# Two passes instead of three for the 64-row token tile of a hybrid trunk, and token reloads behind the last output unit

## The chip, the cores and the metric

The kernel runs on one core of a Trainium2 chip. The metric is the device time of one execution in microseconds, the median over runs. Everything is float32 in memory; the large projections are made of products in the fp32r format, which the code calls a high part and a rest.

## What is computed

One inference step of a one-layer trunk for 512 prompt tokens and 64 sample tokens, model width 1024. Cut to what matters here:

```python
u = rmsnorm(h, g_mix)
proj = u @ w_in                       # q, k, v, LRU input and gate, z, x/B/C, dt (8 columns)
o_a = stick_breaking(q, k, v)         # attention without softmax
o_b = rglru_branch(...)               # gated linear recurrence
o_c = ssd_branch(...)                 # Mamba-2 scan, gated with silu(z)
gates = sigmoid(u @ w_gate + b_gate)
merged = gates[0] * (o_a @ wbo[:512]) + gates[1] * (o_b @ wbo[512:1024]) + gates[2] * (o_c @ wbo[1024:])
h = h + merged @ w_out
h = h + hier_moe(rmsnorm(h, g_ffn))   # router: 1 of 4 groups, 2 of its 8 experts; 32 SwiGLU experts
y = rmsnorm(h, g_final)
```

## The kernel before

The 576 tokens are five tiles (`TT`): four of 128 rows and the last, tile 4, of 64. An operand of a large projection is split on the chip: `u_high_r` is `u` rounded to fp32r and `u_rest_r` what is left; weights likewise (`high_r`, `rest_r`). A product then takes three matmuls for each of the eight 128-row slices `k` of the contraction, in `product` (lines 790 to 794): high by high, high by rest, rest by high.

The projections are one list of work items (`ITEMS`, lines 107 to 130), which TensorE runs in that order into the two banks of `pj`: item n uses bank n % 2 and waits until item n-2 has been drained. The kinds that matter here: `v` (a token tile as the stationary operand, 512 weight columns moving), `z` and `o` (a token tile stationary, 256 columns), `dt` (8 weight columns stationary, 288 tokens moving). Tile 4 has one `v` item, two `z` items and four `o` items, written below as o(4,0) to o(4,3). `DRAINED` says which engine drains: ScalarE takes `v`, `z` and `dt`, VectorE takes `k`, `b` and `o`.

Other steps (`JOBS`) are hung between the items: attention in the stretch of the x, r, gb and z items, then the LRU and SSD mixers, and between the `o` items the second norm (`ffn_norm`), its transposes (`ffn_turn`), the router's logits and the picking of experts. Each engine walks the same list of jobs and items in order, so a VectorE step is behind every VectorE step of earlier items. After the last `o` item come what is left of the routing (`ranks`, `hots`, `table`, `slots`, `weights`), a gather of token rows on the GpSimd queue, and 16 pairs of experts whose matrices stream from HBM.

SyncE's queue (lines 640 to 762) issues the loads: weight units of 128 columns into four ring slots, each issue waiting for the item that frees its slot. Around the `o` items it issues the second four output units (`OUTU` to `OUTU+3`, q = 2 and 3 of the `o` items), the reload of token tile 0, of tiles 1 to 4 (`reload_x`), and the first two gate matrices, in the order

```python
if u == OUTU + 2:
    sp.wait_ge(S["pj_full"], IDX[("g", KD - 1, 1, 2)] + 1)
    reload_x(0)
...
for t in range(1, NT):
    reload_x(t)
...
load("gate", None, 0, EPAIRS)
sp.wait_ge(S["pj_full"], NITEM)
load("up", None, 0, EPAIRS)
```

Each unit that has landed is split by ScalarE (line 1327, high) and VectorE (line 1736, rest). `reload_x` brings the residual rows back into `h`, to which the drain of an `o` item adds (line 1796). GpSimd's `ffn_norm(0)` (line 2541) fetches the row of gains `g_ffn`, which VectorE needs at line 2021.

Of the kernel before, what the change touches and what calls it, by code (L numbers as in the profile page):

```python
# [27 lines left out]
P = 128  # L28
D = 1024
SEQ = 512  # L30
DEC = 64
# [50 lines left out]
SMALL = 1312  # L82
# [48 lines left out]
DVE_KINDS = ("k", "b", "o")  # L131
IDX = {}
# [41 lines left out]
for _it in ITEMS:  # L174
    _e = 1 if _it[0] in DVE_KINDS else 0
    _cnt[_e] += 1
    DRAINED.append((_e, _cnt[_e]))

ATT = [("p", hp, kb) for hp in range(PAIRS) for kb in reversed(range(KB))]
# [105 lines left out]
def trunk_and_experts(nc, a, o):  # L285

    ctx = ExitStack()
    with ctx:
# [124 lines left out]
        xp = [at(x, 584) for x in xp_off]  # L413
        v_sb = at(merged_off, NT, W)
# [41 lines left out]

        wexp_off = front
# [76 lines left out]
        w_dt_h = tiny(KD * 8)  # L534
# [17 lines left out]
        w_dt_hr = region("w_dt_high_r", small, KD * 8).rearrange("p (k n) -> p k n", k=KD)  # L552
        w_dt_rr = region("w_dt_rest_r", w_dt_off, KD * 8).rearrange("p (k n) -> p k n", k=KD)
# [28 lines left out]
        def last_bank(k):  # L582
# [6 lines left out]
            route_ps route_in routed mix_high mix_rest vp_in consts gmix_in ut_u ut_h high_r rest_r v_rest_p wdt_r  # L589
# [51 lines left out]
        def _(sp):  # L641
# [122 lines left out]
        def _(pe):  # L764
# [30 lines left out]

            def item(n):
# [4 lines left out]
                if kind == "v":  # L801

                    pe.wait_ge(S["ut_r"], hh + 1)
                s = SLOT.get(u)
# [19 lines left out]
                elif kind == "o":  # L824
# [4 lines left out]
                    for k in range(KD):  # L829
                        if n == OUT0:  # L830
                            pe.wait_ge(S["mix_rest"], NMIX + 2 * k + 1)
                        mh, mr = (x[k // 2][:, k % 2, o0:o0 + rows_n] for x in (merged_high, merged_rest))
                        m = product(out, (mh, mr), (pair_r(s, 1, k), pair_r(s, 0, k)), k)
                elif kind == "v":
                    o0, rows_n = TT[hh]
                    for k in range(KD):
                        if hh == 0 and k % 2 == 0:
                            j = k // 2
                            pe.wait_ge(*((S["rest_r"], j + 1) if j < NVD else (S["v_rest_p"], j - NVD + 1)))
                        uh, ur = (x[:, k, o0:o0 + rows_n] for x in (u_high_r, u_rest_r))  # L840
                        m = product(bank[0:rows_n, :], (uh, ur), (v_high[:, k, :], v_rest[:, k, :]), k)
                elif kind == "z":
                    o0, rows_n = TT[hh]
                    out = bank[0:rows_n, 0:256].rearrange("p (a b) -> p a b", a=2)
                    for k in range(KD):
# [97 lines left out]
            def att_values(u):  # L943
                kind, hp, kb = ATT[u]
                w = att_a[u % 2]
                if u == 0:
                    wait_drained(pe, IDX[("v", 0, NT - 1)])
                    pe.wait_ge(S["vp_in"], 16)
# [350 lines left out]
        def _(act):  # L1299
# [43 lines left out]
            def params(_):  # L1343
# [3 lines left out]
                act.activation(w_dt_hr, w_dt, ACT.Copy).then_inc(S["wdt_r"], 1)  # L1347
# [4 lines left out]

            def item(n):
                it = ITEMS[n]
                kind, c, hh = it[:3]
                if kind in DVE_KINDS:
# [17 lines left out]
                elif kind == "dt":  # L1374
                    if hh == 0:
                        act.wait_ge(S["xt_ps"], NT)
                    m = act.activation(dtT[0:8, lo:lo + HALF], bank[0:8, 0:HALF], ACT.Copy)
# [30 lines left out]
                if n == IDX[("v", 0, NT - 1)]:  # L1408
                    act.wait_ge(*drained(n))
                    act.dma_start(o["v_p"][0, 0].rearrange("(t p) h d -> p t (h d)", p=P),  # L1410
                                  v_sb[:, 0:NT - 1, :]).then_inc(S["v_out"], 16)
                    act.dma_start(o["v_s"][0, 0].rearrange("s h d -> s (h d)"),
                                  v_sb[0:DEC, NT - 1, :]).then_inc(S["v_out"], 16)
# [275 lines left out]
        def _(dve):  # L1689
# [60 lines left out]
            def params(_):  # L1750
                par_half()
                dve.wait_ge(S["wdt_r"], 1)
                dve.tensor_tensor(w_dt_rr, w_dt, w_dt_hr, ALU.subtract
# [12 lines left out]
            def item(n):  # L1766
                it = ITEMS[n]
                kind, c, hh = it[:3]
                if kind not in DVE_KINDS:
# [3 lines left out]
                lo = hh * HALF  # L1773
                if kind == "k":
# [15 lines left out]
                elif kind == "o":  # L1790
                    t, q = c, hh
                    r = TT[t][1]
                    if q == 0:
# [3 lines left out]
                                                 op0=ALU.mult, op1=ALU.add)  # L1797
                m.then_inc(S["pj_dve"], 1)
# [553 lines left out]
        def _(pool):  # L2352
# [52 lines left out]

            pool.wait_ge(S["xt_ps"], NT)
# [220 lines left out]
```

## Time and profile before

| | |
|---|---|
| median of 3 runs | 1193.73 us (1193.71, 1193.73, 1196.59) |
| the profiled execution's own time | 1197.67 us |
| its span in the profile | 1195.9 us |
| TensorE busy | 1115.6 us (93%) |
| VectorE, ScalarE, GpSimd busy | 532.3, 329.3, 220.7 us |
| mean granted TensorE clock | 0.974 of 2.4 GHz |
| HBM read | 258.24 MB |

Times in the rows are microseconds from the start of the span. The profile models the end of a matmul, so matmuls overlap in it: what one costs is the distance from its start to the next start. A bracket at the end of a row is the idle time before it and what ended that.

### The profile page before, as it was taken

The numbers are of one execution on the slowest core, as the hardware profiler recorded it, in microseconds if no ns is written. First come the engines' busy times: TensorE is split into PE (matmuls) and PEld (weight loads), VectorE is DVE, ScalarE is ACT, GpSimd is POOL, SyncE is SP. The second block draws the span as 40 slices with busy tenths as digits, with TensorE's granted clock in tenths as the row PEclk, the third lists the DMA queues.
The fourth block names the chain that finished last, engine by engine and source line by source line (L and its number), as shares of the span: only waits on it lengthen the run. The fifth ranks groups of instructions, "written<-read, shape, count | busy, mean of one in ns | idle before, by whom it ended". The sixth has DMA issues, their size and how long they took to land.

```text
span 1195.9 us, 16868 instructions
## 1 busy us (share of the span) xinstructions
PE 1115.6 (93%) x6713; PEld 790.2 (66%) x6713; DVE 532.3 (45%) x990; ACT 329.3 (28%) x555; POOL 220.7 (18%) x232
## 2 busy tenths in 40 slices
PE   5999999999999999999999879999999989998994
PEld 4799877779989899999989743344334333333431
DVE  4331787763257555534435631343333333232335
ACT  3323444444366444433321101111111111111113
POOL 6000423333513446532200000000000000000000
PEclk8999999999999999999999869999999999999997
DMA  9278544463312112353280399999999999999982
GB/s 191 77 126 113 51 53 49 52 53 38 94 53 67 59 54 63 89 138 97 76 287 39 147 361 429 401 415 428 428 428 426 426 429 427 427 427 428 427 344 81
DMA packets 93292, 263.15 MB, mean 220 GB/s; under 512 B 5021, under 2 KB 73849, under 8 KB 80937
## 3 DMA queue, kind: packets, MB, share of 16 engines
q1 hardware_dynamic: 86640, 250.36, 61.0%
q0 software_dynamic: 3456, 6.58, 1.7%
q10 hardware_dynamic: 3128, 5.29, 1.2%
q8 instruction: 45, 0.74, 0.2%
q14 instruction: 23, 0.18, 0.0%
HBM read 258.24 MB, written 7.64 MB: 222 GB/s over the span
## 4 chain that ended last, share of the span: by engine, by line
PE 59%; DMA 27%; DVE 7%; ACT 3%; issue 2%; SPq 1%; POOL 0%; ACTq 0%; DVEq 0%; POOLq 0%
DMA arena<-in_w_expert_up 22%; PE za L1165 12%; PE pj L792 11%; PE pj L794 10%; PE pj L793 10%; DMA ring<-in_w_in 3%; PE pj L819 2%; PE zb L1179 2%; DVE arena L1896 1%; DMA ring<-in_w_out 1%; PE ms L1092 1%; DVE arena L1871 1%; PE zb L929 1%; DVE arena L1857 1%; PE zb L1040 1%
## 5 line engine op out<-in xcount | busy, mean ns | idle before, releaser
L1165 PE MATMUL za<-arena 128*64 128x512 f32 x1024 | 233.3, 610 | 23.6 <-DMA arena<-in_w_expert_up 21.6
L792 PE MATMUL pj<-u_high_r,ring_r 128*128 128x288 f32 x736 | 224.0, 304 | 0.1
L794 PE MATMUL pj<-u_high_r,ring_r 128*128 128x288 f32 x736 | 216.8, 295 | 0.0
L793 PE MATMUL pj<-u_rest_r,ring_r 128*128 128x288 f32 x736 | 216.8, 294 | 0.0
L1165 PEld LDWEIGHTS za<-arena 128*64 128x64 f32 x1024 | 73.6, 140 | 174.3 <-issue 140.5
L792 PEld LDWEIGHTS pj<-u_high_r,ring_r 128*128 128x128 f32 x736 | 138.1, 188 | 12.7 <-issue 10.9
L793 PEld LDWEIGHTS pj<-u_rest_r,ring_r 128*128 128x128 f32 x736 | 138.2, 188 | 0.6
L794 PEld LDWEIGHTS pj<-u_high_r,ring_r 128*128 128x128 f32 x736 | 138.1, 188 | 0.0
L1736 DVE TENSOR_TENSOR ring_r<-ring,ring_r 128x1024 fp32r<-128x1024 f32 x62 | 79.8, 1290 | 108.5 <-ACT ring_r L1327 108.5
L1179 PE MATMUL zb<-arena 128*64 128x512 f32 x512 | 113.6, 595 | 3.5 <-DMA arena<-in_w_expert_down 1.0
L1179 PEld LDWEIGHTS zb<-arena 128*64 128x64 f32 x512 | 36.1, 137 | 74.0 <-issue 71.2
L2578 POOL COPY arena<-arena 128x1 int32 (+1 forms) x15 | 2.7, 182 | 379.6 <-PE ms L1157 379.6
L1327 ACT ACTIVATE ring_r<-ring 128x1024 fp32r<-128x1024 f32 x62 | 64.6, 1050 | 21.3 <-DMA ring<-in_w_in 15.9
L2274 DVE SCALAR_TENSOR_TENSOR y_rest<-zb,arena,y_high 128x512 fp32r<-128x512 f32 x32 | 24.0, 750 | 88.6 <-ACT y_high L1612 88.6
L2258 DVE SCALAR_TENSOR_TENSOR arena<-arena,za 128x512 f32<-128x512 f32 x16 | 11.0, 688 | 117.1 <-PE za L1165 117.1
L2230 DVE TENSOR_TENSOR arena<-arena,pj 128x512 f32<-128x512 f32 (+1 forms) x90 | 57.1, 674 | 0.0
L1612 ACT ACTIVATE y_high<-zb,arena 128x512 fp32r<-128x512 f32 x32 | 22.0, 687 | 127.2 <-PE zb L1179 127.2
L2252 DVE SCALAR_TENSOR_TENSOR arena<-arena,za 128x512 f32<-128x512 f32 x16 | 11.0, 688 | 101.4 <-ACT arena L1596 101.4
L1406 ACT ACTIVATE arena<-pj,arena 128x288 f32<-128x288 f32 x48 | 23.9, 498 | 107.0 <-PE pj L794 106.9
L1593 ACT ACTIVATE arena<-oa 128x512 f32<-128x512 f32 x16 | 9.6, 598 | 147.9 <-PE ms L1157 147.9
L2539 POOL TENSOR_TENSOR merged<-merged,arena 128x288 f32<-128x288 f32 x32 | 35.0, 1095 | 81.2 <-DVE arena L1788 80.9
L1596 ACT ACTIVATE arena<-za 128x512 f32<-128x512 f32 x16 | 9.6, 597 | 145.9 <-PE za L1165 145.9
(451 smaller groups left out, 2042.6 us busy)
## 6 DMA issues: line engine op xcount, KB each, us to landing
arena<-in_w_expert_gate SPq DMA_DIRECT2D x32, 2048.0 KB, 25.9
arena<-in_w_expert_up SPq DMA_DIRECT2D x32, 2048.0 KB, 17.8
arena<-in_w_expert_down SPq DMA_DIRECT2D x32, 2048.0 KB, 16.9
ring<-in_w_in SPq DMA_DIRECT2D x26, 512.0 KB, 8.4
ring<-in_w_gate SPq DMA_DIRECT2D x24, 512.0 KB, 4.1
arena<-in_x_prompt SPq DMA_DIRECT2D x8, 512.0 KB, 11.1
ring<-in_w_branch_out SPq DMA_DIRECT2D x8, 512.0 KB, 3.4
ring<-in_w_in SPq DMA_DIRECT2D x2, 1024.0 KB, 12.8
```

The source lines that it names most:

```text
L792: pe.matmul(out, left[0], right[0], start=k == 0, stop=False)
L793: pe.matmul(out, left[0], right[1], start=False, stop=False)
L794: return pe.matmul(out, left[1], right[0], start=False, stop=k == last - 1)
L819: m = pe.matmul(bank[:, 0:HALF], ring4[s][:, k, m_cols], oAT[:, k, cols], start=k == 0, stop=k == WT - 1)
L1165: m = pe.matmul(za[j * BLK:(j + 1) * BLK, b, :], xT[spare][:, k, j * BLK:(j + 1) * BLK], w[:, j * KD + k, :], start=k == 0, stop=k == KD - 1)
L1179: m = pe.matmul(zb[j * BLK:(j + 1) * BLK, q, :], hidT[:, k, j * BLK:(j + 1) * BLK], w[:, j * (DE // P) + k, q * 512:(q + 1) * 512], start= ...
L1327: act.activation(high_r[s], raw[s], ACT.Copy).then_inc(S["high_r"], 1)
L1406: m = act.activation(gsb[k % 2], bank[:, 0:HALF], ACT.Tanh, scale=0.5, bias=cpar[:, j:j + 1])
L1736: dve.tensor_tensor(rest_r[s], raw[s], high_r[s], ALU.subtract).then_inc(S["rest_r"], 1)
L2230: dve.tensor_tensor(v, v, add_bank(k)[0:n, :], ALU.add).then_inc(S["sc_r"], 1)
L2274: dve.scalar_tensor_tensor(out=y_rest[:, half], in0=zb[:, q, :], scalar=weight_now, in1=y_high[:, half], op0=ALU.mult, op1=ALU.subtract).t ...
L2539: pool.tensor_tensor(v, v, gtmp[k % 2], ALU.add).then_inc(S["gm_r"], 1)
```

## The change

Tile 4 fills only 64 of 128 stationary columns. The new kernel puts the high part of its 64 rows into columns 0 to 63 of a packed operand and the rest into columns 64 to 127 (`u_pack` for `v` and `z`, `merged_pack` for `o`), and `two_passes` runs it against the high and the rest weights: two matmuls for each slice in place of three. Rows 0 to 63 of the bank then hold the high part's products, rows 64 to 127 those of the rest (rest by rest is now included), so the drain has two halves: ScalarE copies the upper rows out, VectorE adds the lower ones. `dt` is packed the other way: 8 high and 8 rest weight columns are one stationary operand of 16, and `dt_turn` sums the two halves in a small matmul with `dt_sel` where it was a transpose. GpSimd copies the packed operands: two copies of 128x512 elements for `u_pack` and eight of 128x128 for `merged_pack`, the latter ahead of the fetch of `g_ffn`. SyncE waits for the last output unit's landing before it reloads token tiles 1 to 4, and so before the first gate matrices.

```diff
@@ SyncE
                 sp.dma_start(dst, src.rearrange("(k p) n -> p k n", p=P)).then_inc(unit_in[SLOT[u]], 16)
+            last_out = SLOT[OUTU + 3]
+            sp.wait_ge(unit_in[last_out], 16 * ARRIVAL[OUTU + 3])
             for t in range(1, NT):
                 reload_x(t)
@@ TensorE
+            def two_passes(out, both, right, k):
+
+                pe.matmul(out, both, right[0], start=k == 0, stop=False)
+                return pe.matmul(out, both, right[1], start=False, stop=k == KD - 1)
...
+                if packed(it):
+                    pe.wait_ge(S["pack_r"], 10 if kind == "o" else 2)
...
+                    if packed(it):
+                        out = bank[:, 0:256].rearrange("p (a b) -> p a b", a=2)
+                        for k in range(KD):
+                            m = two_passes(out, merged_pack[:, k, :], (pair_r(s, 1, k), pair_r(s, 0, k)), k)
...
-                        m = product(bank[0:8, 0:HALF], (w_dt_hr[:, k, :], w_dt_rr[:, k, :]),
-                                    (u_high_r[:, k, cols], u_rest_r[:, k, cols]), k)
+                        m = two_passes(bank[0:16, 0:HALF], w_dt_pack[:, k, :],
+                                       (u_high_r[:, k, cols], u_rest_r[:, k, cols]), k)
...
-                    m = pe.transpose(ms[0:n, t * 8:t * 8 + 8], dtT[0:8, o0:o0 + n], ident[0:8, 0:8])
+                    m = pe.matmul(ms[0:n, t * 8:t * 8 + 8], dtT[0:16, o0:o0 + n], dt_sel[0:16, :], start=True, stop=True)
@@ ScalarE
+                if packed(it):
+
+                    act.wait_ge(S["pj_full"], n + 1)
...
+                        dst, half = out_part[0:DEC, :], 0.5
+                        if hh > 0:
+                            wait_drained(act, n - 1)
+                    act.activation(dst, pj[DEC:P, n % 2, 0:w], ACT.Copy, scale=half).then_inc(S["high_sum_r"], 1)
+                    if n == IDX[("v", 0, NT - 1)]:
+                        store_values(n)
+                    return
@@ VectorE
+                if kind in "vz":
+                    dve.wait_ge(S["high_sum_r"], PACKED[n])
+                    dst = v_sb[0:DEC, hh, :] if kind == "v" else z2[0:DEC, hh, 256 * c:256 * (c + 1)]
+                    m = dve.scalar_tensor_tensor(out=dst, in0=bank[0:DEC, 0:512 if kind == "v" else 256], scalar=1.0 if kind == "v" else 0.5,
+                                                 in1=dst, op0=ALU.mult, op1=ALU.add)
...
+                    if packed(it):
+                        link(m)
+                        dve.wait_ge(S["high_sum_r"], PACKED[n])
+                        m = dve.tensor_tensor(v, v, out_part[0:r, :], ALU.add)
@@ GpSimd
+            pool.wait_ge(S["ut_r"], NT)
+            for j, src in enumerate((u_high_r, u_rest_r)):
+                pool.tensor_copy(u_pack[:, :, j * DEC:(j + 1) * DEC], src[:, :, SEQ:T]).then_inc(S["pack_r"], 1)
...
+                    pool.wait_ge(S["mix_rest"], NMIX + 2 * KD)
+                    for j, parts in enumerate((merged_high, merged_rest)):
+                        for i, src in enumerate(parts):
+                            pool.tensor_copy(merged_pack[:, 2 * i:2 * i + 2, j * DEC:(j + 1) * DEC],
+                                             src[:, :, SEQ:T]).then_inc(S["pack_r"], 1)
                     pool.wait_ge(S["gm_r"], 4 * KD)
```

On SyncE, around the last output units, before:

```order
L645 DMA arena<-in_x_prompt 128x1024 [waits pj_full]
L685 DMA ring<-in_w_out 128x8x128
L685 DMA ring<-in_w_out 128x8x128 [waits pj_full]
L645 DMA arena<-in_x_prompt 128x1024 x3
L645 DMA arena<-in_x_sample 64x1024
L700 DMA arena<-in_w_expert_gate 128x4096 [waits tl_out,so_out,gm_r]
```

and now:

```order
L658 DMA arena<-in_x_prompt 128x1024 [waits pj_full]
L698 DMA ring<-in_w_out 128x8x128
L698 DMA ring<-in_w_out 128x8x128 [waits pj_full]
L658 DMA arena<-in_x_prompt 128x1024 [waits unit_in1]
L658 DMA arena<-in_x_prompt 128x1024 x2
L658 DMA arena<-in_x_sample 64x1024
L715 DMA arena<-in_w_expert_gate 128x4096 [waits tl_out,so_out,gm_r]
```

The order is the same; tiles 1 to 4 and the gate matrices now stand behind a wait for the last unit.

On VectorE, from the norm of tile 3 through the drains of o(4,0) and o(4,1), before (line 1796 is the drain, lines 2040 to 2072 pick tile 2's first expert, 2021 is tile 3's norm):

```order
L2021 SCALAR_TENSOR_TENSOR arena<-arena 128x1024 [waits dve_c]
L1796 SCALAR_TENSOR_TENSOR arena<-pj,arena 64x256 [waits x_in4,pj_full]
L2040 TENSOR_REDUCE arena<-arena 128x1
L2041 TENSOR_TENSOR arena<-arena 128x32 [waits dve_c]
L2042 TENSOR_TENSOR arena<-arena 128x32 [waits dve_c]
L2043 TENSOR_REDUCE arena<-arena 128x1 [waits dve_c]
L2044 TENSOR_TENSOR arena<-arena 128x32 [waits dve_c]
L2072 SCALAR_TENSOR_TENSOR arena<-arena 128x32 [waits dve_c]
L1796 SCALAR_TENSOR_TENSOR arena<-pj,arena 64x256 [waits pj_full,dve_c]
```

and now:

```order
L2087 SCALAR_TENSOR_TENSOR arena<-arena 128x1024 [waits dve_c]
L1858 SCALAR_TENSOR_TENSOR arena<-pj,arena 64x256 [waits x_in4,pj_full]
L1863 TENSOR_TENSOR arena<-arena 64x256 [waits high_sum_r,dve_c]
L2106 TENSOR_REDUCE arena<-arena 128x1
L2107 TENSOR_TENSOR arena<-arena 128x32 [waits dve_c]
L2108 TENSOR_TENSOR arena<-arena 128x32 [waits dve_c]
L2109 TENSOR_REDUCE arena<-arena 128x1 [waits dve_c]
L2110 TENSOR_TENSOR arena<-arena 128x32 [waits dve_c]
L2138 SCALAR_TENSOR_TENSOR arena<-arena 128x32 [waits dve_c]
L1858 SCALAR_TENSOR_TENSOR arena<-pj,arena 64x256 [waits pj_full,dve_c]
L1863 TENSOR_TENSOR arena<-arena 64x256 [waits high_sum_r,dve_c]
```

Each drain is followed by an addition that waits for ScalarE's copy (`high_sum_r`) and for the drain itself.

On GpSimd, after the last addition to `merged`, now (before, the fetch of `g_ffn` followed it directly):

```order
L2608 TENSOR_TENSOR merged_57<-merged_57,arena 128x288 [waits pj_dve] x4
L2617 COPY merged_pack<-merged_high_62 128x2x64 [waits mix_rest]
L2617 COPY merged_pack<-merged_high_63 128x2x64
...
L2617 COPY merged_pack<-merged_rest_61 128x2x64
L2621 DMA arena<-in_g_ffn 128x1024 [waits so_out,gm_r]
```

Eight copies, the first behind a wait for VectorE's last split of `merged`, now stand ahead of the fetch.

## Rows read from the trace of the kernel before

**Rows 1.** The page's chain that ended last, shares by engine.

```profile
PE 59%; DMA 27%; DVE 7%; ACT 3%; issue 2%; SPq 1%; POOL 0%; ACTq 0%; DVEq 0%; POOLq 0%
```

**Rows 2.** Timelines (start us, us, engine line): v item of tile 4.

```profile
44.94 0.69 DVE L1724 TENSOR_TENSOR u_rest_r<-u_rest,u_high_r 128x512 fp32r<-128x512 f32 x1 [0.69 <-ACT u_high_r L1317]
...
50.56 0.40 PE L792 MATMUL pj<-ring_r,u_high_r 128*64 128x512 f32 x1
...
55.85 0.39 PE L794 MATMUL pj<-ring_r,u_rest_r 128*64 128x512 f32 x1
```

**Rows 3.** Timeline of TensorE: first and last slice of the two dt items.

```profile
112.34 0.29 PE L792 MATMUL pj<-u_high_r,w_dt_high_r 128*8 128x288 f32 x1
...
118.21 0.29 PE L792 MATMUL pj<-u_high_r,w_dt_high_r 128*8 128x288 f32 x1
```

**Rows 4.** Timeline of TensorE: last two slices of tile 4's first z.

```profile
305.37 0.28 PE L792 MATMUL pj<-ring_r,u_high_r 128*64 128x256 f32 x1
...
305.71 0.28 PE L792 MATMUL pj<-ring_r,u_high_r 128*64 128x256 f32 x1
```

**Rows 5.** Timeline of TensorE: end of o(0,2), start of o(0,3).

```profile
611.63 0.28 PE L793 MATMUL pj<-ring_r,merged_high 128*128 128x256 f32 x1
611.75 0.28 PE L794 MATMUL pj<-ring_r,merged_rest 128*128 128x256 f32 x1
614.91 0.36 PE L792 MATMUL pj<-ring_r,merged_high 128*128 128x256 f32 x1 [2.88 <-DVE ring_r L1736]
```

**Rows 6.** Timelines of ScalarE, VectorE and SyncE's queue around that stop.

```profile
612.45 1.06 ACT L1327 ACTIVATE ring_r<-ring 128x1024 fp32r<-128x1024 f32 x1 [4.06 <-DMA ring<-in_w_out]
...
606.43 2.35 DVE L1736 TENSOR_TENSOR ring_r<-ring,ring_r 128x1024 fp32r<-128x1024 f32 x2
...
602.05 1.54 SPq L685 DMA_DIRECT2D ring<-in_w_out  x2
603.63 2.67 SPq L645 DMA_DIRECT2D arena<-in_x_prompt  x3
...
607.07 1.18 SPq L700 DMA_DIRECT2D arena<-in_w_expert_gate  x2
```

**Rows 7.** DMA issues from 585 to 640 us: KB each, median us to landing.

```profile
arena<-in_w_expert_gate SPq DMA_DIRECT2D x2, 2048.0 KB, 19.8
...
ring<-in_w_out SPq DMA_DIRECT2D x3, 512.0 KB, 5.3
...
arena<-in_g_ffn POOLq DMA_DIRECT2D x1, 512.0 KB, 7.6
```

**Rows 8.** Line 1736 (min/median/max ns), GpSimd's cast, its g_ffn issue, VectorE's first use.

```profile
L1736 DVE TENSOR_TENSOR ring_r<-ring,ring_r x62: 1212/1225/2300, 65.4 to 613.5; 128x1024 fp32r<-128x1024 f32 x62
...
L2411 POOL CAST sum_high<-arena 128x256 fp32r<-128x256 f32 x4 | 2.5, 632 | 109.7 <-PE za L929 109.7
...
604.86 0.62 POOL L2547 DMA_DIRECT2D arena<-in_g_ffn  x1 [0.30 <-POOL merged L2539]
...
621.41 1.28 DVE L2021 SCALAR_TENSOR_TENSOR arena<-arena 128x1024 f32<-128x1024 f32 x1
```

**Rows 9.** Timelines of VectorE and TensorE in tile 4's o items and behind.

```profile
665.28 0.41 DVE L1796 SCALAR_TENSOR_TENSOR arena<-pj,arena 64x256 f32<-64x256 f32 x1
...
673.66 0.42 DVE L1796 SCALAR_TENSOR_TENSOR arena<-pj,arena 64x256 f32<-64x256 f32 x1 [1.16 <-PE pj L794]
...
676.85 0.42 DVE L1796 SCALAR_TENSOR_TENSOR arena<-pj,arena 64x256 f32<-64x256 f32 x1 [0.78 <-PE pj L794]
...
668.82 1.98 PE L1092 MATMUL ms<-arena 128*128 128x36 f32 x16 [1.11 <-ACT arena L1584]
678.77 0.64 PE L1227 MATMUL oa<-arena 128*128 128x32 f32 x2 [2.03 <-DVE arena L2084]
```

**Rows 10.** Granted clock by stretch (us, engines' busy times, PEclk, DMA share, GB/s).

```profile
612.00:616.00 4.00, 1.12 (x10) 1.12 (x10) 1.56 (x2) 1.06 (x1) 0.00 (x0) 1.00 1.14 272
...
680.00:690.00 10.00, 6.56 (x40) 6.20 (x40) 7.96 (x32) 1.88 (x2) 1.52 (x2) 0.50 1.00 415
```

More of the change, by code:

```diff
@@ L81 @@
 TAILS = 80
-SMALL = 1312
+SMALL = 1040
 ARENA = 53200
@@ L131, with packed @@
 DVE_KINDS = ("k", "b", "o")
+def packed(it):
+    return it[0] in ("v", "z", "o") and (it[1] if it[0] == "o" else it[2]) == NT - 1
 IDX = {}
@@ L174 @@
 for _it in ITEMS:
-    _e = 1 if _it[0] in DVE_KINDS else 0
+    _e = 1 if _it[0] in DVE_KINDS or packed(_it) else 0
     _cnt[_e] += 1
     DRAINED.append((_e, _cnt[_e]))
+PACKED = {i: n + 1 for n, i in enumerate(i for i, it in enumerate(ITEMS) if packed(it))}
 ATT = [("p", hp, kb) for hp in range(PAIRS) for kb in reversed(range(KB))]
@@ L413, in trunk_and_experts @@
         xp = [at(x, 584) for x in xp_off]
+        u_pack = region("u_pack", cut[0], KD * P).rearrange("p (k n) -> p k n", k=KD)
+        assert cut[0] + KD * P <= ARENA
         v_sb = at(merged_off, NT, W)
@@ L454, in trunk_and_experts @@
         out_high = [None, mixed("lru_high", gb_off, F32R), mixed("ssm_high", q2_off, F32R)]
+        merged_pack = region("merged_pack", front + 8192, KD * P).rearrange("p (k n) -> p k n", k=KD)
+        out_part = at(ARENA - 256, 256)
         wexp_off = front
@@ L532, in tiny @@
             return at(cs[0] - n, *dims)
-        w_dt_h = tiny(KD * 8)
+        w_dt_pack_off = cs[0]
+        tiny(KD * 16)
+        dt_sel = tiny(8)
         ssq = tiny(8)
@@ L551, in trunk_and_experts @@
         w_r = tiny(KD, 36)
-        w_dt_hr = region("w_dt_high_r", small, KD * 8).rearrange("p (k n) -> p k n", k=KD)
-        w_dt_rr = region("w_dt_rest_r", w_dt_off, KD * 8).rearrange("p (k n) -> p k n", k=KD)
+        w_dt_pack = region("w_dt_pack", w_dt_pack_off, KD * 16).rearrange("p (k n) -> p k n", k=KD)
         w_sel = tiny(NT, 2)
@@ L828, in item @@
                     out = bank[0:rows_n, 0:256].rearrange("p (a b) -> p a b", a=2)
-                    for k in range(KD):
+                    if packed(it):
+                        out = bank[:, 0:256].rearrange("p (a b) -> p a b", a=2)
+                        for k in range(KD):
+                            m = two_passes(out, merged_pack[:, k, :], (pair_r(s, 1, k), pair_r(s, 0, k)), k)
+                    for k in range(0 if packed(it) else KD):
                         if n == OUT0:
@@ L840, in item @@
                         uh, ur = (x[:, k, o0:o0 + rows_n] for x in (u_high_r, u_rest_r))
+                        if packed(it):
+                            m = two_passes(bank, u_pack[:, k, :], (v_high[:, k, :], v_rest[:, k, :]), k)
+                            continue
                         m = product(bank[0:rows_n, :], (uh, ur), (v_high[:, k, :], v_rest[:, k, :]), k)
@@ L844, in item @@
                     out = bank[0:rows_n, 0:256].rearrange("p (a b) -> p a b", a=2)
-                    for k in range(KD):
+                    if packed(it):
+                        out = bank[:, 0:256].rearrange("p (a b) -> p a b", a=2)
+                        for k in range(KD):
+                            m = two_passes(out, u_pack[:, k, :], (pair_r(s, 1, k), pair_r(s, 0, k)), k)
+                    for k in range(0 if packed(it) else KD):
                         uh, ur = (x[:, k, o0:o0 + rows_n] for x in (u_high_r, u_rest_r))
@@ L947, in att_values @@
                     wait_drained(pe, IDX[("v", 0, NT - 1)])
+                    wait_drained(pe, IDX[("v", 0, NT - 2)])
                     pe.wait_ge(S["vp_in"], 16)
@@ L1351, in params, with store_values @@
                 act.activation(cst, oa[:, 0:NST], ACT.Copy).then_inc(S["par_up"], 1)
+            def store_values(n):
+                for i in range(n + 1):
+                    if i > n - 2:
+                        wait_drained(act, i)
+                wait_drained(act, IDX[("v", 0, NT - 2)])
+                act.dma_start(o["v_p"][0, 0].rearrange("(t p) h d -> p t (h d)", p=P),
+                              v_sb[:, 0:NT - 1, :]).then_inc(S["v_out"], 16)
+                act.dma_start(o["v_s"][0, 0].rearrange("s h d -> s (h d)"),
+                              v_sb[0:DEC, NT - 1, :]).then_inc(S["v_out"], 16)
             def item(n):
@@ L1355, in item @@
                 kind, c, hh = it[:3]
+                if packed(it):
+                    act.wait_ge(S["pj_full"], n + 1)
+                    w = 512 if kind == "v" else 256
+                    if kind == "v":
+                        dst, half = v_sb[0:DEC, hh, :], 1.0
+                    elif kind == "z":
+                        if c == 0:
+                            act.wait_ge(S["dt_ps"], 1)
+                        dst, half = z2[0:DEC, hh, 256 * c:256 * (c + 1)], 0.5
+                    else:
+                        dst, half = out_part[0:DEC, :], 0.5
[5 more added lines that the diff above has]
+                    return
                 if kind in DVE_KINDS:
@@ L1407, in item @@
                 m.then_inc(S["pj_act"], 1)
[L1408 to L1413, printed above, removed]
             def keys_out(t):
@@ L1752, in params @@
                 dve.wait_ge(S["wdt_r"], 1)
-                dve.tensor_tensor(w_dt_rr, w_dt, w_dt_hr, ALU.subtract
+                dve.tensor_tensor(dt_sel, ident[:, 0:8], ident[:, 8:16], ALU.add)
+                dve.tensor_tensor(w_dt_pack[:, :, 8:16], w_dt, w_dt_pack[:, :, 0:8], ALU.subtract
                                   ).then_inc(S["wdt_r"], 1)
@@ L1768, in item @@
                 kind, c, hh = it[:3]
-                if kind not in DVE_KINDS:
+                if kind not in DVE_KINDS and not packed(it):
                     return
@@ L1797, in item @@
                                                  op0=ALU.mult, op1=ALU.add)
+                    if packed(it):
+                        link(m)
+                        dve.wait_ge(S["high_sum_r"], PACKED[n])
+                        m = dve.tensor_tensor(v, v, out_part[0:r, :], ALU.add)
                 m.then_inc(S["pj_dve"], 1)
```

6 lines of the change are left out of this document (3 added, 3 removed).

## The prediction

> **What bounds the kernel now.** I read the chain of waits first: TensorE holds 59% of it and transfers 27% [rows 1]. The transfers on it are mostly the expert matrices at the end; the projections, which this change touches, are TensorE's. Then I read the timelines of TensorE at the places where the change removes matmuls. The reader should see there starts at an even distance with no bracket, so a matmul that goes takes its distance with it, as long as nothing late stands behind it. The two exceptions are the stop ahead of o(0,3) [rows 5] and the `o` items of tile 4, where TensorE and VectorE wait for each other [rows 9].
>
> All sums are made against the profiled execution, 1197.67 us (span 1195.9). The median of the three runs, 1193.73, lies 3.9 us below it, and I subtract from that. About 0.3%, 3.6 us, is what a measurement of this kernel can tell from no change.
>
> **The v item of tile 4.** Its 24 matmuls start from 50.56 to 55.85 [rows 2]: 23 steps, 0.230 us each. Sixteen remain: 8 x 0.230 = 1.8 us saved. The moving operand is unchanged, so I keep the step. Its new input is ready in time: the rest of tile 4 is done at 44.94 + 0.69 = 45.6, and GpSimd's two copies of 512 elements have until 50.56, 4.9 us. Its cast of 256 elements took 0.63 us on average [rows 8], so two copies of twice that are an estimated 2.5 us. VectorE's extra addition and ScalarE's copy run under the next item, which lasts longer than the copy and the addition together. The loads that this item's end releases start earlier with it, so the stage moves as a whole.
>
> **dt.** From the first to the last slice, 15 slices of three matmuls take 118.21 - 112.34 = 5.87 us [rows 3], 0.130 us a matmul. Of 48, 16 go: 2.1 us. The five small matmuls that now replace transposes may cost some 0.1 us in all. I count 2.0.
>
> **z.** Two items. A slice takes 305.71 - 305.37 = 0.34 us [rows 4], an item 8 x 0.34 = 2.72. With 128 stationary columns the step is 611.75 - 611.63 = 0.12 us [rows 5], an item 16 x 0.12 = 1.92. That is 0.8 each, 1.6 us. The drain moves from ScalarE alone to ScalarE and VectorE, and the next step in each queue starts from the same item's end, so I count nothing for it.
>
> **The stop ahead of o(0,3).** TensorE issued at 611.75 and next at 614.91, waiting for VectorE's split of the last output unit [rows 5]. ScalarE began its half of that split at 612.45 after 4.06 us of waiting for the transfer [rows 6]. The unit was issued at about 603.2, right before tiles 1 to 3 and, from 607.07, the first gate matrices [rows 6]; it took 9.2 us, where such a unit's median is 5.3 [rows 7]. Without that company it should land between 608.5 (5.3) and 610 (its neighbour ahead of it in the queue first). ScalarE needs 1.06 and VectorE 1.23, and the latter still has the unit before in its queue, so the operand is there at about 612.3. Two bounds. If the transfer is as late as before, the gain is nothing. If it is early, o(0,3) starts at 611.87 and the gain is 3.0.
>
> GpSimd's eight copies take something back. They start when the last split of `merged` is done, about when VectorE begins its two splits at 606.43 (2.35 us for both, [rows 6]). Line 1736 took 1.225 us in the median and 2.300 at most [rows 8]; the long ones lie beside GpSimd's work. So o(0,2), whose operand is the second of these, is late by between 0 and 2.15 us. The copies are short and cover about half of the two splits: I take 0.5, nearest to the lower row, and o(0,3) starts at 612.5. Gain 2.4 us, bounds -0.2 and 3.0.
>
> The Trainium skill's page "SBUF — State Buffer", section "Who interferes with whom", says that a VectorE instruction with two SBUF inputs contends with a GpSimd instruction that reads SBUF, and that the pair of ports is an exclusive lock. The long rows of line 1736 agree. Read strictly, all eight copies would stand in VectorE's way and the gain here would be 0.7 in place of 2.4.
>
> **Tile 4's o items.** TensorE loses 4 x 0.8 = 3.2 us, but VectorE is the longer queue here. It drained o(4,0) at 665.28 without any wait, right behind tile 3's norm [rows 9], so an earlier matmul does not bring this forward. Each drain now has an addition of another 64x256 behind it, linked: 0.41 us for the drain's like [rows 9], 0.45 with the link. Working the two queues through from these rows (the times are estimates): the drain of o(4,1) is 0.45 late, its end 0.9 late; tile 2's second pick ends 0.9 late, at about 670.2. ScalarE's copy of o(4,1) waits for the first addition (666.1), done by 666.6; its copy behind tile 3's transposes then lets TensorE start the logits at 668.05, not 668.82, and o(4,2) is done at 671.9. So VectorE drains o(4,2) at 672.05, not 673.66: the waits of 1.16 and 0.78 us shrink. With the picks between them unchanged, o(4,3) is fully added at 675.7 where the old drain ended its queue slot at 677.2. I count 1.5 us; bounds are 3.2 (VectorE is no limit) and -0.5 (1.0 us for each addition, from ScalarE's hand-over, less the waits).
>
> **What is moved and costs nothing.** Tiles 1 to 4 are issued from about 610; tile 1 is first needed at the drain of o(1,0), near 619.6. The first gate matrices are issued some 5 us later than 607.07, and with their 19.8 us to landing [rows 7] are there by 633; nobody reads them before the routing is over, past 700. The up matrices wait for the last `o` item, which is earlier. `g_ffn` is behind the copies: issued at about 605.6 + 8 x 0.32 (half of the 0.632 for half the elements) = 608.2 where it was 604.86, with 7.6 us to landing [rows 7] there at about 616.4. It is needed at 621.41 - 2.4 = 619.0 [rows 8]. If it shared its fate with the gate matrices (19.8), it would be there at 628, 9 us late.
>
> **Sum:** 1.8 + 2.0 + 1.6 + 2.4 + 1.5 = 9.3 us. Nothing behind the routing has a date of its own; the experts' stream starts from the gather. So 1197.67 becomes 1188.4, and the median 1193.7 becomes **1184.4 us**.
>
> **Rivals.**
> - *The unit lands late anyway.* For it: SyncE's queue is full of small rows, and tile 0's reload is still ahead of the unit. Against it: 9.2 against 5.3 us. The stop stays, tiles 1 to 4 follow still later: 2.4 less, 1186.8.
> - *TensorE's clock falls in tile 4.* With less work per item TensorE waits more there: some 1.6 us ahead of the logits, where it was 1.11 [rows 9]. For it: the wait of 2.03 at 678.77 was followed by a stretch at 0.50, the lower of the two levels, 1.2 GHz [rows 9, 10]. Against it: the stop ahead of o(0,3) left the clock at 1.00 [rows 10]. The logits and two items, 1.8 + 2 x 1.92 us, would double: up to 5.6 more, of which VectorE's queue hides about 1. The time would be 1189.0. The Trainium skill's page "TensorE: Matmul & The Clock Gate", section "What's actually happening", has it that the throttled state is the default and activity releases it; rows here show both outcomes after a wait.
> - *g_ffn arrives behind the gate matrices* (slower). VectorE stands at line 2021 for tile 0, and behind it the drains of o(1,0) and all that follow. For it: the fetch now starts with the reloads and the gate matrices, not ahead of them. Against it: it was issued among the reloads before and took 7.6. It decides once the row lands later than 619.0 + 9.3 = 628.3. With each copy at 0.632 us (5.1 for the eight) and 19.8 to landing it lands at 605.6 + 5.1 + 19.8 = 630.5, 11.5 late: 1195.9, still within 0.3%; it passes that bound, 1197.3, if the row lands another 1.4 us later.
> - *The packing doesn't do what it says* (more than two passes a slice): the matmul counts exclude it.
>
> **How the numbers follow.** All terms as worked out: 0.64. Late unit: 0.12. Clock: 0.09. Little gained, by several costs at their bounds: 0.10. `g_ffn`: 0.05, of which 0.02 past 1197.3. The bounds of the likeliest case: at best 1.8 + 2.1 + 1.6 + 3.0 + 3.2 = 11.7, 1182.0; at worst, with the late unit and tile 4 at its bound, 5.4 - 0.2 - 0.5 = 4.7, 1189.0. Together with the clock's case and half a microsecond of spread between runs the range is 1181.5 to 1190.5. Faster by over 0.3% means below 1190.1, which is all of the first three cases: 0.85; within it is little gained and most of `g_ffn`: 0.13; slower: 0.02.
>
> **What would show it.** In the profile after: 16 matmuls in each packed item; tile 4's `v` near 3.7 us and `z` near 1.9; dt near 4.2 from first to last; no bracket, or a short one, ahead of o(0,3); the first gate matrices issued behind the last unit's landing; the last VectorE drain 1.5 us earlier against the end of o(3,3). A bracket at the first line-2021 row's place naming `g_ffn`, or a granted clock below 1.00 between o(4,0) and o(4,3), would make the prediction wrong.

## The result, and the profile after

| | before | after |
|---|---|---|
| median (least to most, runs) | 1193.73 us (1193.56 to 1198.04, 5) | 1186.51 us (1185.45 to 1188.15, 5) |
| the profiled execution's own time, its span | 1197.67, 1195.9 us | 1185.46, 1183.6 us |
| TensorE busy | 1115.6 us | 1105.3 us |

The ratio of the changed kernel's time to that of the kernel before is 0.993 with a 95% interval of 0.991 to 0.995. Ratios below are of the same kind, each against executions of the kernel before on the same chip, with the interval in brackets. In a second series the changed kernel (a_again below) had 0.9926 (0.9913 to 0.9939). Of 1193.7 us the two ratios take off 8.4 and 8.8 us; the medians differ by 7.2. Forecast were 9.3 us less, 1184.4, with a range of 1181.5 to 1190.5.

The spans of the two profiled executions lie 12.3 us apart. 4.0 of that is not the change's: TensorE's clock came to its upper level earlier, before any changed step, and r0 below, which has the kernel before's code up to there, starts tile 4's `v` at 46.89 us. Windows of both kernels over that stretch and over a second one that matters below, before and then after (us, busy times by engine, granted clock, DMA share, GB/s):

```profile
20.00:48.00 28.00, 24.28 (x98) 19.21 (x98) 13.68 (x20) 10.45 (x18) 8.25 (x9) 0.82 0.52 119
```

```profile
20.00:48.00 28.00, 24.98 (x115) 20.18 (x116) 13.69 (x20) 11.39 (x20) 9.09 (x11) 0.94 0.52 121
...
657.00:660.00 3.00, 3.00 (x15) 3.00 (x16) 1.83 (x12) 0.00 (x0) 0.84 (x2) 0.50 0.00 0
```

The chain that ended last reads much as in [rows 1]:

```profile
PE 64%; DMA 25%; DVE 6%; ACT 2%; issue 2%; SPq 1%; POOL 0%; DVEq 0%; POOLq 0%; ACTq 0%
```

So the trace has to be read by distances, place by place. Starts of TensorE's matmuls in both traces:

| place | before | after | gained there |
|---|---|---|---|
| first matmul of tile 4's v | 50.56 | 46.56 | (4.0, not the change) |
| v: to the first work behind it | 5.52 | 3.73 | 1.8 |
| dt: to the next x item | 6.78 | 4.72 | 2.1 |
| z: to the next item, both | 3.94, 2.73 | 3.09, 1.89 | 0.85, 0.84 |
| start of o(0,2) to start of o(0,3) | 5.98 | 2.94 | 3.0 |
| start of o(1,0) to last matmul of o(4,3) | 58.61 | 57.45 | 1.2 |
| from there to the last matmul of all | 504.5 | 506.0 | -1.5 |

Timelines of TensorE after, for v, dt and the first z of tile 4 (first and last matmul, answering to [rows 2 to 4]; the columns are those of rows 2):

```profile
46.56 0.40 PE L813 MATMUL pj<-ring_r,u_pack 128*128 128x512 f32 x1
...
50.06 0.40 PE L814 MATMUL pj<-ring_r,u_pack 128*128 128x512 f32 x1
...
106.42 0.29 PE L813 MATMUL pj<-u_high_r,w_dt_pack 128*16 128x288 f32 x1
...
110.50 0.29 PE L814 MATMUL pj<-u_rest_r,w_dt_pack 128*16 128x288 f32 x1
...
295.13 0.39 PE L813 MATMUL pj<-ring_r,u_pack 128*128 128x256 f32 x1
...
296.96 0.28 PE L814 MATMUL pj<-ring_r,u_pack 128*128 128x256 f32 x1
```

The steps are nearly those of before (0.233, 0.132 and 0.12 us, where it was 0.230, 0.130 and 0.114), there are only fewer of them.

Around the last output units (timelines of SyncE's queue, ScalarE, VectorE, GpSimd and TensorE after, answering to [rows 5, 6]):

```profile
592.37 1.54 SPq L698 DMA_DIRECT2D ring<-in_w_out  x2
599.33 1.29 SPq L658 DMA_DIRECT2D arena<-in_x_prompt  x3
601.25 1.07 SPq L715 DMA_DIRECT2D arena<-in_w_expert_gate  x2
...
599.33 1.06 ACT L1361 ACTIVATE ring_r<-ring 128x1024 fp32r<-128x1024 f32 x1 [0.70 <-DMA ring<-in_w_out]
...
596.75 2.48 DVE L1792 TENSOR_TENSOR ring_r<-ring,ring_r 128x1024 fp32r<-128x1024 f32 x2
608.75 1.28 DVE L2087 SCALAR_TENSOR_TENSOR arena<-arena 128x1024 f32<-128x1024 f32 x1
...
595.92 1.01 POOL L2617 CAST merged_pack<-merged_high 128x128 fp32r<-128x128 f32 x4 [1.03 <-DVE merged_rest L1797]
596.87 2.99 POOL L2617 CAST merged_pack<-merged_rest 128x128 fp32r<-128x128 f32 x4
599.81 0.62 POOL L2621 DMA_DIRECT2D arena<-in_g_ffn  x1
...
602.32 0.28 PE L807 MATMUL pj<-ring_r,merged_high 128*128 128x256 f32 x1
```

The bracket ahead of o(0,3) is gone. The reloads stand behind the unit's landing, and the fetch of `g_ffn`, issued at 599.81, goes out after the second reload and ahead of the gate matrices; with 6.7 us to landing it is there 2.3 us before line 2087 wants it.

Tile 4's `o` items after (timelines of TensorE and VectorE, answering to [rows 9]):

```profile
655.10 2.07 PE L1126 MATMUL ms<-arena 128*128 128x36 f32 x16 [1.25 <-ACT arena L1640]
...
657.34 0.41 PE L814 MATMUL pj<-ring_r,merged_pack 128*128 128x256 f32 x1
657.55 0.41 PE L813 MATMUL pj<-ring_r,merged_pack 128*128 128x256 f32 x1
...
660.69 0.42 DVE L1858 SCALAR_TENSOR_TENSOR arena<-pj,arena 64x256 f32<-64x256 f32 x1 [1.51 <-PE pj L814]
663.60 0.42 DVE L1858 SCALAR_TENSOR_TENSOR arena<-pj,arena 64x256 f32<-64x256 f32 x1
```

The matmuls of o(4,2) stand 0.21 us apart, not 0.12: in the window 657 to 660 above the granted clock is 0.50, the lower of its two levels. VectorE waits 1.51 us for them.

### The profile page after: what moved, and what is told of

It reads as the page before. It is cut to its first block, busy times and chain, and to the rows that moved or that the text cites. A ratio compares the mean times of both kernels' runs of the same rounds, so it can differ in the third digit from the quotient of the medians.

```text
span 1183.6 us, 16768 instructions
## 1 busy us (share of the span) xinstructions
PE 1105.3 (93%) x6646; PEld 783.2 (66%) x6646; DVE 534.7 (45%) x998; ACT 331.2 (28%) x559; POOL 224.8 (19%) x242
## 4 chain that ended last, share of the span: by engine, by line
PE 64%; DMA 25%; DVE 6%; ACT 2%; issue 2%; SPq 1%; POOL 0%; DVEq 0%; POOLq 0%; ACTq 0%
DMA arena<-in_w_expert_up 22%; PE za L1199 13%; PE pj L807 12%; PE pj L808 11%; PE pj L809 11%; PE pj L841 2%; PE zb L1213 2%; DMA ring<-in_w_in 2%; DVE arena L1962 1%; PE pj L813 1%; PE zb L962 1%; PE pj L814 1%; PE ms L1126 1%; PE zb L1074 1%; DMA arena<-u2d,arena 1%
```

## Experiments

### e1 and e2: the packing without the wait, and the wait without the packing

e1 takes these two lines out of the changed kernel, e2 puts them into the kernel before:

```diff
             last_out = SLOT[OUTU + 3]
             sp.wait_ge(unit_in[last_out], 16 * ARRIVAL[OUTU + 3])
```

> The changed kernel without SyncE's wait for the last output unit. Theory (the wait is what lets that unit land early): the stop ahead of o(0,3) is back, 2 to 3.3 us with VectorE's split of the unit as its releaser, and the time is 1186.5 + 3.0 = 1189.5 us. Rival (the unit's late landing in the kernel before was chance, or the shifted order of the packed kernel cures it): no stop, 1186.5 us.

> The kernel before with SyncE's wait alone, nothing packed. Theory: the stop ahead of o(0,3) goes, 3.0 us, and nothing else moves: 1193.7 - 3.0 = 1190.7 us. Rival (the gain there belongs to the packing): the stop stays and the time is 1193.7 us.

Measured: e1 has a ratio of 0.9977 (0.9959 to 0.9994), 2.7 us below before; e2 has 1.0003 (0.9986 to 1.0019). Neither theory stands as written. In e1 no stop comes back ahead of o(0,3): the unit lands in 5.8 us without the wait. What comes is another one, 10 us later (e1's timelines of VectorE and TensorE, then of its DMA issues the row with KB each and us to landing, then the window behind the stop):

```profile
612.04 1.28 DVE L2085 SCALAR_TENSOR_TENSOR arena<-arena 128x1024 f32<-128x1024 f32 x1 [3.59 <-DMA arena<-in_g_ffn]
...
613.38 0.92 PE L1113 MATMUL za<-arena 128*128 128x128 f32 x6 [2.54 <-DVE arena L2085]
```

```profile
arena<-in_g_ffn POOLq DMA_DIRECT2D x1, 512.0 KB, 12.4
```

```profile
614.00:617.50 3.50, 3.50 (x19) 3.50 (x18) 0.00 (x0) 1.02 (x1) 0.00 (x0) 0.51 0.49 187
```

The eight copies push the fetch to 599.53, and without the wait the gate matrices have left at 596.86, ahead of it. That is the prediction's slower rival, at 12.4 us to landing where it was priced with 19.8. Behind the stop TensorE's granted clock is 0.51 for 3.5 us; together they make the way from o(1,0) to o(4,0) 4.27 us longer (47.63 us, where the changed kernel has 43.35). In e2 the stop ahead of o(0,3) is gone from the profile (o(0,2) to o(0,3) 2.95 us), yet the ratio shows no gain: the 3.0 us of the theory would be 0.9975, which lies outside the interval. r0 below has the kernel before's code up to there and no wait, and its profile has no stop either (2.94). So the 2.88 us of [rows 5] belong to the execution that was profiled, not to every one; how many have them is not known.

### e3 and g2: o left at three passes

e3 is the changed kernel with `o` taken out of `packed` and without the eight copies; g2 adds a wait of GpSimd ahead of the fetch:

```diff
-    return it[0] in ("v", "z", "o") and (it[1] if it[0] == "o" else it[2]) == NT - 1
+    return it[0] in ("v", "z") and it[2] == NT - 1
...
+                    pool.wait_ge(unit_in[SLOT[OUTU + 3]], 16 * ARRIVAL[OUTU + 3])
```

> The changed kernel with the four o items of tile 4 left at three passes, without GpSimd's eight copies and VectorE's additions; v, z and dt stay packed and the wait stays. Theory (TensorE's clock fell in o(4,2) and took back what packing o had gained): the granted clock is 1.00 through tile 4, ranks of tile 3 start at about the same distance from o(1,0) as in the changed kernel (60.8 us, against 60.9 before), and the time is 1185.8 to 1186.6 us. Rival (packing o is worth the 1.5 us that were forecast): 1188.0 us.

> e3 (v, z, dt packed, o in three passes, SyncE's wait) with the fetch of g_ffn behind the last output unit's landing too. Theory: the stop of 1.8 us that e3 showed ahead of o(0,3) goes, the unit lands within 6 us of its issue, the fetch lands before VectorE needs it; 1.8 us below e3, about 1188.3 us. Rival: the unit takes 8 us as in e3, 1190.1 us.

Measured: e3 has 0.9954 (0.9935 to 0.9973), 5.5 us below before; g2 has 0.9959 (0.9945 to 0.9974), 4.9 us. So v, dt and z are worth some 5 us, against 5.5 in the table above, and packing `o` is worth the rest: beside g2 on the same chip the changed kernel had 0.9926 (0.9913 to 0.9939), the intervals don't meet, and the medians lie 3.3 us apart (1188.16 and 1184.89). The theory that packing `o` had earned next to nothing falls; its 1.2 us in the table are what a fall of the clock left. In e3's profile the clock fell too, with three passes, against what was expected, and the last unit took 8.1 us with a stop of 1.78:

```profile
605.04 0.36 PE L807 MATMUL pj<-ring_r,merged_high 128*128 128x256 f32 x1 [1.78 <-DVE ring_r L1792]
```

In e3 SyncE's wait held the reloads and the gate matrices back until that unit had landed, so they are not what made it late there. g2's unit took 5.7 us and there was no stop, but its ratio is e3's: the late landing, too, comes and goes.

### g1 and a_again: the fetch ahead of the copies

g1 moves the three lines of the fetch of `g_ffn` ahead of the copies; a_again is the changed kernel beside it.

```diff
+                    pool.wait_ge(S["gm_r"], 4 * KD)
+                    pool.wait_ge(S["so_out"], 32)
+                    pool.dma_start(g_ffn, a["g_ffn"][0:1, :].partition_broadcast(P)).then_inc(S["gains_in"], 16)
                     pool.wait_ge(S["mix_rest"], NMIX + 2 * KD)
```

> The changed kernel with the fetch of g_ffn ahead of GpSimd's eight copies, so issued 4 us earlier, while the last output unit is under way. Theory (what made that unit late is the fetch of g_ffn beside it, as in the kernel before and in e3): a stop of 1 to 3 us ahead of o(0,3) in the profile, and 1 to 2 us more than the changed kernel. Rival (the tile reloads and gate matrices made it late, and SyncE's wait cures that): no stop, the same time as the changed kernel.

> The changed kernel once more, beside the kernels of this series. Every theory: the same ratio to the kernel before as at first, 0.991 to 0.995. What the profile should tell: whether the granted clock falls in o(4,2) again (theory: the wait ahead of tile 3's logits leaves it to chance, since e3 had that wait of 1.1 us and a fall, the kernel before the same wait and none).

Measured: g1 has 0.9945 (0.9933 to 0.9958), 1186.50 us, against 1184.89 of a_again. Its profile shows no stop: the unit lands in 5.8 us with the fetch beside it. The medians lie 1.6 us apart as the theory had it, but the intervals meet. Whether the fetch is what makes that unit late in some executions stays open.

### e4: TensorE's wait ahead of tile 3's logits filled

```diff
+                if t == NT - 2:
+                    for _ in range(10):
+                        pe.matmul(za[:, 0, 0:256].rearrange("p (a b) -> p a b", a=2), merged_pack[:, 0, :],
+                                  pair_r(SLOT[OUT_EARLY], 1, 0), start=True, stop=True)
                 pe.wait_ge(S["u2t_r"], t + 1)
```

> The changed kernel with ten matmuls of 256 columns, whose sums nobody reads, between tile 3's transposes and its logits, where TensorE waits 1.25 us. Theory (that wait is what let the clock fall): the granted clock stays at 1.00 until o(4,3) is done, o(4,2) takes 1.9 us from its first to its last matmul instead of 3.3, VectorE's last drain is some 1.4 us earlier, and the time is 1185.1 us. Rival (VectorE's queue is the limit there anyway): o(4,2) is shorter, the last drain is not earlier, 1186.5 us. Second rival (the clock falls whatever TensorE does in that wait): o(4,2) still takes 3.3 us.

Measured: the ratio is 0.9915 (0.9893 to 0.9937), the median 1184.68 us, not to be told from a_again. Its TensorE and windows:

```profile
655.78 1.44 PE L1126 MATMUL za<-early_r,merged_pack 128*128 128x256 f32 x10
657.27 1.98 PE L1130 MATMUL ms<-arena 128*128 128x36 f32 x16
659.08 0.36 PE L813 MATMUL pj<-ring_r,merged_pack 128*128 128x256 f32 x1
```

```profile
655.00:659.00 4.00, 3.94 (x34) 3.74 (x34) 3.56 (x16) 1.41 (x2) 0.00 (x0) 1.00 0.32 131
659.00:661.00 2.00, 2.00 (x19) 2.00 (x19) 1.76 (x9) 0.00 (x0) 0.84 (x2) 1.00 0.00 0
```

o(4,2) now takes 1.87 us from first to last matmul, and VectorE's last drain starts 57.40 us behind o(1,0), where it was 58.40: 1.0 us earlier, against 1.4 expected. All profiles together, from the start of o(1,0) to the last matmul of o(4,3) in us, tell what `o` is worth and what the clock takes:

| | clock stays at 1.00 | clock falls in o(4,2) |
|---|---|---|
| o in three passes | 58.61 (before, e2, r0), 58.54 (g2) | 60.28 (e3) |
| o packed, wait as it is | 55.91 (g1) | 57.45 (after), 57.46 (a_again), 57.43 (r1), 57.48 (e1, its 4.27 taken out; the fall runs on into o(4,3)) |
| o packed, wait filled | 55.91 (e4), 55.92 (e6), 55.89 (r2), 55.93 (r3) | none |

Up to TensorE's last matmul packing `o` is worth 2.7 us with the clock up. The fall takes 1.5 of it back (1.7 with three passes), in four of five packed profiles whose wait is not filled, in one of five with three passes, and in none of four with the wait filled. The waits were 1.25 and 1.11 us, and g1 had the wait of 1.25 and no fall: which execution falls is not settled by the wait's length alone.

Behind the `o` items the routing goes by VectorE's queue, and there packing gains less. The gather of the first expert's rows is issued, in the kernel before, the changed kernel and g1 (timelines of GpSimd; o(1,0) starts at 617.86, 605.20 and 605.48):

```profile
695.60 1.10 POOL L2584 DMA_INDIRECT arena<-u2d,arena  x1 [8.89 <-POOLq L2580]
682.82 1.10 POOL L2658 DMA_INDIRECT arena<-u2d,arena  x1 [8.90 <-POOLq L2654]
682.10 1.10 POOL L2658 DMA_INDIRECT arena<-u2d,arena  x1 [8.90 <-POOLq L2654]
```

From the start of o(1,0) that is 77.7, 77.6 and 76.6 us: packing `o` brings the gather forward by 0.1 us with the fall and by 1.1 without it. Of the other profiles e2, r0 and g2 agree with the first within 0.1 us, a_again and r1 with the second, e4 and r3 with the third; e1 lies between (76.9 with its 4.27 taken out), e3 has three passes and the fall (79.4).

### e6: every wait behind o(4,3) filled, too

44 matmuls of 512 float32 columns on top of e4, ahead of `ranks`, `ffn_turn`, `logits`, `table`, `weights` and the first rows' transposes.

```diff
+            def keep_busy(bank, n):
+                for _ in range(n):
+                    pe.matmul(bank, ident, arena[:, 0:512], start=True, stop=True)
```

> e4 with further matmuls whose sums nobody reads (44 of 512 columns in all) in TensorE's waits from o(4,3) to the first expert's rows. Theory (the clock at its lower level from tile 4's routing to the first expert costs time there): the granted clock stays at 1.00 up to the experts, tile 4's logits take 1.0 us instead of 1.9, the first gate's first 5 us run at full clock, the hole in the transfers between 680 and 690 us closes, and the time is 2 to 3 us below e4, about 1182 us. Rival (the experts' stream has its own pace): as e4, 1184.7 us. Second rival (the extra matmuls stand in the way of the routing's): above e4.

Measured: the ratio is 1.0051 (1.0037 to 1.0065), the median 1200.51 us: the second rival. Up to 700 us the clock stays at 1.00 but for a stretch between 683 and 687, but a float32 matmul of 512 columns takes 0.87 us (two rows of the trace each), where one in fp32r takes 0.23. Eleven of them fill a wait of 3.0 us with 9.6:

```profile
661.60 9.60 PE L1267 MATMUL za<-arena 128*128 128x512 f32 x22
671.04 0.30 PE L1274 MATMUL oa<-arena 128*128 128x32 f32 x2
```

### r0 and r1: the first up matrices 10 us earlier

In every profile so far but e6's the gather of the first expert's rows landed 0.5 to 1.3 us behind 8 MB of up and gate matrices. r0 is the kernel before with this edit, r1 the changed kernel with it and with `merged_pack` in four other places.

```diff
-            sp.wait_ge(S["pj_full"], NITEM)
+            sp.wait_ge(S["pj_full"], NITEM - 2)
             load("up", None, 0, EPAIRS)
+            sp.wait_ge(S["pj_full"], NITEM)
             load("gate", None, 1, 1 + EPAIRS, 1)
```

> The kernel before, with SyncE's wait ahead of the first up matrices cut from the last o item to o(4,1), whose units are the last that those matrices overwrite; the second gate matrices still wait for o(4,3). Theory (behind o(4,3) it is not VectorE's queue that sets the time, but 8 MB of up and gate matrices, 25.4 us from their issue in every run, with the gather of the first expert's rows landing 0.5 to 1.3 us behind the last of them): the gather lands within 5 us of its issue instead of 7.3, the first expert starts 2 to 3 us earlier against the end of o(4,3), and the time is about 2.5 us less than before, 1191 us. Rival (the routing sets it): no change, 1193.7 us.

> The changed kernel with the same earlier issue; merged_pack moves to four places of 256 columns that the up matrices don't overwrite. Theory: 2.5 us below the changed kernel, ratio to the kernel before 0.990 to 0.991, about 1182.5 us. Rival: no change, ratio 0.9926.

Measured: r0 has 0.9999 (0.9981 to 1.0017), r1 has 0.9928 (0.9907 to 0.9949): the rival both times. The transfers did move as the theory had it: the gather takes 4.4 us instead of 7, and in r0 the down matrices leave 2.9 us earlier against SyncE's first issue behind o(4,3) (SyncE's queue, the kernel before and then r0):

```profile
676.78 0.80 SPq L700 DMA_DIRECT2D arena<-in_w_expert_up  x2
702.91 0.80 SPq L700 DMA_DIRECT2D arena<-in_w_expert_down  x2
...
661.53 0.95 SPq L700 DMA_DIRECT2D arena<-in_w_expert_up  x2
671.45 1.67 SPq L700 DMA_DIRECT2D arena<-in_w_expert_gate  x2
694.67 0.80 SPq L700 DMA_DIRECT2D arena<-in_w_expert_down  x2
```

That is 702.91 - 676.78 = 26.1 us before and 694.67 - 671.45 = 23.2 in r0. From the end of o(4,3) to the last matmul it is 506.45 us in r0 and 506.53 in r1 all the same, with 504.5 to 506.4 in the kernels above, e6 aside: what was won is gone by the end of the expert stage. Where it goes was not followed.

### r2 and r3: filling of the right size

r2 is r1 with e4's filling and 24 float32 matmuls of 256 columns in e6's places; r3 has the filling alone.

> r1 with the ten filling matmuls of e4, and 24 of 256 columns in float32 (0.43 us each at the upper clock, a quarter to a half of the waits they stand in) in place of e6's 44 of 512 columns (0.87 us each, which by e6's trace were longer than the waits) from o(4,3) to the first expert's rows. Theory (with the transfers out of the way, the routing and the first expert at the lower clock are what is left): o(4,2) takes 1.9 us, the clock stays at 1.00 into the first expert, and the time is 2 to 4 us below r1, 1179 to 1180.5 us. Rival (the stream of expert matrices takes back what the routing gains): as r1. Second rival (the filling still stands in the way): above r1.

> The changed kernel with r2's filling matmuls alone: merged_pack and the up matrices where the change has them. Theory (the earlier up matrices earn nothing, as r0 and r1 showed; the clock does): the clock stays at 1.00 into the first expert, and the time is r2's, ratio 0.9907 to the kernel before, about 1183.4 us. Rival (the filling pays only where the gather is not held up behind 8 MB of matrices): the first rows still land 26 us after the issue of the up matrices, and the ratio is e4's, 0.9915, or the changed kernel's, 0.9926.

Measured: r2 has 0.9907 (0.9887 to 0.9928), 1183.38 us; r3 has 0.992 (0.9899 to 0.9941), 1184.47 us. Both miss what the theories had, 1179 to 1180.5 us and r2's ratio, though r3's interval takes in 0.9907. All six times of r2 (1182.42 to 1184.24) lie below all six of r1 (1184.32 to 1187.15) on the same chip, 2.9 us by the medians, so the filling earns something there; but r2's interval meets the changed kernel's. In r2's trace the third pair of gate matrices leaves 33.6 us behind the last matmul of o(4,3) (695.70 - 662.08), where after had 39.7 (702.37 - 662.65); from that matmul to the last of all it is 504.4 us, 1.6 less than after, but the kernel before has 504.5 there without any filling, so that of those 6.1 us any arrives is not shown. (r3 has 503.4, the least of all.) r2 is the lowest median of the study and is not shown to beat the change. r2's clock fell between 672 and 677 only (0.66), r3's was at 0.55 from 670 to 680 in spite of the filling:

```profile
670.00:680.00 10.00, 9.82 (x41) 8.71 (x40) 6.76 (x37) 0.73 (x2) 1.52 (x2) 0.55 1.00 415
```

## Why the prediction held, point by point

- **v, dt, z**: 1.8, 2.0 and 1.6 us were forecast, 1.8, 2.1 and 1.7 are in the trace, and the times of g2 and e3 have 4.9 and 5.5 for the three together. Counting the matmuls that go, times the distance between two starts, was right.
- **The stop ahead of o(0,3)**: 2.4 us were forecast, 3.0 are in the pair of traces, and the ratio of e2 shows nothing of them. This is the step that failed: "Without that company it should land between 608.5 and 610" took the reloads and gate matrices for the cause, and one execution's late landing for the kernel's. e1 and r0 show the unit in time (5.8 us) with all its company, e3 shows it late (8.1 us) without the company that SyncE's wait holds back. What makes it late stays open.
- **GpSimd's copies**: 0.5 us were counted for VectorE's two splits beside them. They took 2.48 us against 2.35 [rows 6], so 0.13; the copies gave way: four took 1.01 us ahead of the splits, four 2.99 beside them. The Trainium skill's page "SBUF — State Buffer", section "Who interferes with whom", adds that issue order decides who blocks; of its strict reading in the prediction (0.7 in place of 2.4) nothing is seen.
- **Tile 4's o items**: 1.5 us were forecast because VectorE's queue was held to be the limit. In that queue it comes to 1.1 with the clock up (g1, by the issue of the gather) and to 0.1 with the fall, which four of five packed profiles have. TensorE's last matmul moved by 2.7 and 1.2, and by the times packing `o` earned more than forecast, 3.3 (g2 against a_again). So VectorE's queue alone does not account for what packing `o` is worth, and "the experts' stream starts from the gather" does not hold as a measure of the time either: in r0 the gather landed 2.9 us earlier against o(1,0) (82.1 us behind it, before 85.0) and the time did not move. What sets the time behind o(4,3) is not shown.
- **What was costed at nothing**: the fetch of `g_ffn` was in time with about the margin worked out, 2.3 us where it was 619.0 - 616.4 = 2.6; without the wait it would not have been. The wait, which was counted for the output unit, earns its place by keeping the gate matrices behind that fetch: e1 lies 5.6 to 6.1 us above the changed kernel by the ratios (0.9977 against 0.993 and 0.9926), and its profile has 4.27 of that.
- **Rivals**: the clock's, at 0.09, came true in four of the five packed profiles whose wait is not filled. The text had named a clock below 1.00 between o(4,0) and o(4,3) as a sign that would make it wrong; the sign came, at 1.5 us and not at the 4.6 that it was priced with, because the fall covered o(4,2) alone. The `g_ffn` rival came true where the wait was taken out. The late unit's price, 1186.8 us, lies nearest to the measured 1186.51, but not by its mechanism: in the changed kernel's profiles the unit was in time (5.8 and 5.9 us), and so it was in two of three profiles without the wait.
- **The sum**: 9.3 us were forecast; the profiles have 5.5 for v, dt and z and 1.2 to 2.7 for `o`, so 6.7 to 8.2, and the stop in some executions; 7.2 to 8.8 were measured. That the forecast came so near is in part luck: the 2.4 us of the stop are not seen in the times, and `o` earned more than was counted. The upper bound of the range is not the sum given for it, either: 1189.0 and half a microsecond are 1189.5, not 1190.5; the result lies below both. Behind o(4,3) the two traces differ by 1.5 us the other way, within what kernels with the same code there differ by (504.5 to 506.5).

## What to carry to other kernels

A packed operand costs its place in a queue before it costs time: eight small copies ahead of one DMA issue put that transfer behind 4 MB, and the wait that repairs this is part of the packing's price. A stop read from one execution is a term only if a second profile of the same code has it. Matmuls that are put into a wait to keep TensorE's clock up have to be measured first and cut to the wait's length, and a microsecond won ahead of a stream paced by transfers may not reach its end.

## What the runs showed of the hardware that was not expected

- Behind waits of 1.1 to 1.25 us TensorE's granted clock fell to 0.50 in o(4,2) in five of ten profiles, and in none of four with ten matmuls in the wait. The Trainium skill's page "TensorE: Matmul & The Clock Gate", section "What's actually happening", has activity as what releases the throttle; e4 agrees (1.00 from 655 to 661); g1, whose wait is not filled, kept 1.00 as well.
- A float32 matmul of 512 columns and 128 stationary ones took 0.87 us at the upper clock (e6), one in fp32r 0.23 (tile 4's `v` after).
- A gather of 128 rows took 4.4 to 4.5 us when all expert matrices issued ahead of it had landed (r0, r1, r2, e6) and 5.5 to 7.6 when they had not.
- Stretches with the same code differ between executions by more than some terms of this change: the first 50 us by 3.7 (before and r0, 50.56 and 46.89 at tile 4's `v`), the last output unit's landing by 3.4 (5.8 and 9.2 us, the same two).
